# Evictions issued ahead of the background step of a half, and one more step in the gated delta output

## What is computed

```python
def reference(x, ...):                 # x: (1, 256, 2048)
    # block 1
    proj = rms_norm(x) @ w_in          # latent q, kv, rope key, window q/k/v
    h = x + concat(mla_attention(...), swa_sink_attention(...)) @ w_out
    h = h + square(relu(rms_norm(h) @ w_up)) @ w_down          # 2048 -> 8192 -> 2048
    x = rms_norm(h, final_norm)
    # block 2
    proj = rms_norm(x) @ w_in_2        # qkv, z, gates b and a, glu
    o = chunk_gated_delta_rule(q, k, v, g, beta)               # 8 heads of 128
    o = rms_norm(o) * silu(z)
    c = silu(layer_norm(depthwise_conv31(glu)))
    h = x + concat(o, c) @ w_out_2
    h = h + memory_cross_attention(rms_norm(h), rms_norm(mem)) # q, k, v, o: 2048 x 2048
    h = h + square(relu(rms_norm(h) @ w1)) @ w2
    return rms_norm(h)
```

## Time and profile before

| | us |
|---|---|
| median of 3 runs (2673.2 to 2673.64) | 2673.62 |
| the profiled execution | 2671.96 |
| its span, first to last instruction | 2670.2 |
| PE busy in it | 2611.9 |
| DVE busy | 1627.5 |
| ACT busy | 1353.3 |
| mean granted TensorE clock | 0.994 of full |

### The profile page before, as it was taken

One profiled execution on the slowest core, in us unless ns is written; L12 is line 12 of the kernel. 1 busy time (PEld: TensorE's weight loads), 2 busy tenths in 40 slices (PEclk: granted clock), 3 DMA queues, 4 the chain that ended last, 5 costly groups with the idle time before them and its releaser, 6 DMA issues. The chain is left out here.

```text
span 2670.2 us, 31500 instructions
## 1 busy us (share of the span) xinstructions
PE 2611.9 (98%) x12544; PEld 2168.4 (81%) x12544; DVE 1627.5 (61%) x1992; ACT 1353.3 (51%) x1916; POOL 0.2 (0%) x4
## 2 busy tenths in 40 slices
PE   8999999999999999998899999999999999999998
PEld 7877888888888887887888887888888888888886
DVE  6685555555555556567887856644555555555555
ACT  5554544444444446578867644444544444444443
POOL 0000000000000000000000000000000000000000
PEclk9999999999999999999999999999999999999999
DMA  6533665556655654654443327544465566556553
GB/s 219 159 135 134 219 191 192 188 188 190 192 188 187 190 194 151 199 167 157 129 165 113 133 95 267 175 157 143 162 207 189 185 191 194 187 184 192 195 188 134
DMA packets 235241, 468.70 MB, mean 176 GB/s; under 512 B 8187, under 2 KB 17110, under 8 KB 233814
## 3 DMA queue, kind: packets, MB, share of 16 engines
q1 hardware_dynamic: 234806, 466.16, 53.5%
q10 hardware_dynamic: 288, 0.52, 0.1%
HBM read 460.36 MB, written 6.29 MB: 175 GB/s over the span
## 5 line engine op out<-in xcount | busy, mean ns | idle before, releaser
L138 DVE TENSOR_TENSOR WL<-Wt,WH 128x1024 fp32r<-128x1024 f32 (+1 forms) x862 | 1041.7, 1210 | 802.8 <-ACT WH L135 744.1
L135 ACT ACTIVATE WH<-Wt 128x1024 fp32r<-128x1024 f32 (+1 forms) x862 | 898.7, 1046 | 802.7 <-PE ps L168 797.4
L168 PE MATMUL ps<-WH,XT 128*128 128x512 f32 (+1 forms) x3392 | 1087.8, 394 | 4.6 <-DVE WL L138 4.3
L168 PE MATMUL ps<-WH,HT 128*128 128x512 f32 (+2 forms) x3392 | 1059.7, 389 | 2.5 <-DVE WL L138 2.5
L168 PEld LDWEIGHTS ps<-WH,XT 128*128 128x128 f32 x3392 | 638.6, 189 | 136.8 <-DVE WL L138 5.1
L168 PEld LDWEIGHTS ps<-WH,HT 128*128 128x128 f32 x3392 | 636.2, 188 | 128.3 <-DVE WL L138 3.5
L168 PE MATMUL ps<-WL,XT 128*128 128x512 f32 (+1 forms) x1696 | 660.0, 389 | 0.0
L168 PE MATMUL ps<-WL,HT 128*128 128x512 f32 (+2 forms) x1696 | 655.0, 386 | 0.0
L168 PEld LDWEIGHTS ps<-WL,XT 128*128 128x128 f32 x1696 | 320.3, 189 | 62.5 <-issue 1.0
L168 PEld LDWEIGHTS ps<-WL,HT 128*128 128x128 f32 x1696 | 319.7, 189 | 61.5 <-issue 1.0
L138 DVE TENSOR_TENSOR H<-H,ps 128x512 f32<-128x512 f32 x144 | 92.5, 683 | 26.7 <-PE ps L168 26.7
(11 more groups left out here) (262 smaller groups left out, 1301.8 us busy)
## 6 DMA issues: line engine op xcount, KB each, us to landing
Wt<-in_mlp_w SPq DMA_DIRECT2D x128, 1024.0 KB, 5.3
Wt<-in_w_up SPq DMA_DIRECT2D x64, 1024.0 KB, 5.4
Wt<-in_w_down SPq DMA_DIRECT2D x64, 1024.0 KB, 5.0
Wt<-in_w_in SPq DMA_DIRECT2D x53, 1024.0 KB, 5.1
Wt<-in_w_out SPq DMA_DIRECT2D x32, 1024.0 KB, 5.1
Wt<-in_xa_wk SPq DMA_DIRECT2D x16, 1024.0 KB, 5.1
Wt<-in_xa_wv SPq DMA_DIRECT2D x16, 1024.0 KB, 5.0
Wt<-in_xa_wq SPq DMA_DIRECT2D x16, 1024.0 KB, 5.0
```

Source lines behind the costliest of these rows:

```text
L135: return self.p.act.do(lambda e: e.activation(out, in_, func, **kw), w, self.name + "_a")
L138: return self.p.dve.do(lambda e: e.tensor_tensor(out, a, b, op), w, self.name + "_v")
L168: return self.p.pe.do(lambda e: e.matmul(out, l, r, start=start, stop=stop), w, self.name + "_t" if sig else None)
```

## The change

The call of `evac` moves from behind the loop over halves into it, ahead of `pump()`, in the last half of a chunk's last segment. `gen_o` gets one more `yield` between the gate multiply and its transposes.

```diff
@@ gemm
                 pe_free[i] = tok
+                if last_seg and k2 == kb - 2:
+                    gfree[gs] = evac(ci, c0, w, [G[gs][tb][:, 0:w] for tb in range(2)], tok)
                 pump()
-            if last_seg:
-                gfree[gs] = evac(ci, c0, w, [G[gs][tb][:, 0:w] for tb in range(2)], tok)
         return tok
@@ gen_o
         if b == 0:
             return
+        yield
         st = Stage(p, "turn_o")
```

## The result

| | us |
|---|---|
| before, median of 5 runs (2672.04 to 2673.64) | 2673.2 |
| after, median of 5 runs (2805.5 to 2807.98) | 2806.1 |
| ratio, 95% interval | 1.0501 (1.0489 to 1.0513) |
| the profiled execution of after, its span | 2807.63, 2805.8 |

The change makes the kernel 5.0% slower, 133 us; the forecast was 2806. The two profiled executions differ by 2807.63 - 2671.96 = 135.7 us.

A forecast was written before the change was run, and what follows sets the result against it. PE bounds the kernel, busy 2611.9 of 2670.2 us. Terms sum to 109.6 us, 132.0 with the clock; 2671.96 + 132.0 = 2804.0, forecast as a 2806 us median (runs' median 1.7 above the profiled execution), range 2770 to 2845.

The forecast's parts named there:

- The mechanism: Evictions issued ahead of the background step lose the half that covered them, so PE waits in order at the transposes.
- Up chunks: MLP up chunks: transposes of `Vm` wait for the second square, 2.36 us each, 32 chunks, 75.5 us.
- The other chunks: Stalls at `w_out` and `xo` 13.0 us, `w_out_2` 7.0, queries 4.4, last down product of the first MLP 9.3.
- the third rival: Faster: early evictions let transposes and XS work start earlier in the middle of the kernel; at most 2645 us, chance 0.03.
- The clock: After stalls PE's clock can fall, about 1.6 us each; 14 falls of 36 gaps, 22.4 us, bounds 0 and 57.6.
- every gap falls: Rival: every PE gap of 2.2 us or more is followed by a clock fall; 2842 us, chance 0.12.
- the clock holds: Rival: the same stalls on PE but no clock fall; 2784 us, chance 0.12.
- The input product of block 2: `QB` transposes lose 2.76 us of cover, eviction gains 2.28; net 0.48 for 5 chunks, 2.4 us, bounds -10 to +14.
- the eviction is relieved of the background step that stood ahead of it: At `QB`, the early eviction no longer queues on DVE behind `AC` and `QE`, saving 2.28 us.
- The delta output: `VT` transposes: one more half of cover, less `KVS` put ahead; wait from 4.49 to 2.47 us, -2.0 us.
- the DVE queue would stay as it was but for `KVS` put ahead: At the `VT` transposes, early eviction `KVS` adds 0.74 us while the added half takes 2.76 off the wait.
- The short products: Short q and kv products, grouped with all other evictions: same work in another order, 0 us, bounds -5 to +6.

The follow-up runs named there:

- part 2 alone: Against the kernel before: only the added `yield`, one more step ahead of the transposes of `VT`, evictions not moved; 2668.03 us (ratio 0.9984).

## Why the prediction was right, and where it was not

**The mechanism** was right and is shown: the stalls come with the lost half and go with one step, while the order of the evictions stays (2806.1, 2668.4).

**Up chunks**, 2.36 us each, 75.5 in all: the MLP without falls gives 2.34, and 50.1 + 50.2 - 16 x 1.57 = 75.2 in all. The sum of the three parts read from one place of the timeline (slot, end of the eviction, 0.15 us from DVE to PE) held for all 32: the idle times lie between 2.15 and 2.19 us, 2.20 forecast.

**The other chunks**: `w_out` 6.3 us for four (6.5 forecast); `xo` 8.4 - 1.57 = 6.8 (6.5; one of its four stalls is longer, an idle time of 2.46 us, and the fall follows that one); `w_out_2` 5.9 (7.0, here the `XKB` transposes that stand ahead of two of the four fill part of the stall, which I left out); queries 4.9 (4.4, an eviction that ends 0.94 us behind the slot, although the third rival says that the rows show 1.3 to 2.2); last down product of the first MLP 13.1 - 2 x 1.57 = 10.0, of which 0.9 are a wait for `H` that came behind the first matmul of the next product before, so 9.1 (9.3).

**The clock**: 19 more falls, as long as 20, at 1.57 us: 31.4 us, against 14 at 1.6, 22.4. The price was right and the count was not; it was a choice, and the rows on which it rested did not carry it. The limit between 1.91 and 2.13 us that the prediction drew is not there. In the MLPs one half of the stalls fell (16), where I took two in five; three of the four longer ones did, and one in `xo`. The trace of before had more to say than the rows that I chose: behind its first 100 us PE has eight idle times of more than 2 us (2.13, 2.26, 2.38, 2.79, 2.99, 3.22, 3.57 and 4.49 us), and a fall comes with seven of them, all but the one of 3.22. Taken as a rate that speaks for the rival in which every gap falls, so that the choice of two in five came near the half that was measured is luck. The granted clock came out at 0.982, forecast 0.985. The case "every gap falls" did not occur, nor did "the clock holds". The rule that gave the former, of the Trainium skill, page "TensorE: Matmul & The Clock Gate", Part 4, that transposes do not count as busy PE as matmuls do, is not what this kernel shows: 18 transposes in each stall kept the clock at 1.00.

**The input product of block 2**: +7.5 us where 2.4 were forecast. Three falls' worth of it, 4.7 us, is the clock: the fall behind the last down product's fourth stall, and three of its own, as long as four, where before has two. The term itself was for `QB`, and there the waits came out at 9.4 us instead of 10.3, 0.9 less where 2.4 more were forecast. The step that failed is "the eviction is relieved of the background step that stood ahead of it". The generators too start one half earlier, so the long steps `AC` and `QE` keep their place ahead of `QB`. The DVE queue of after, ahead of one `QB`:

```profile
1304.22 1.22 DVE L138 TENSOR_TENSOR AC<-AC,PRD 128x1024 f32<-128x1024 f32 x1
1305.36 1.22 DVE L149 SCALAR_TENSOR_TENSOR QE<-QA,QE 128x1024 f32<-128x1024 f32 x1
1306.49 1.22 DVE L138 TENSOR_TENSOR WL<-Wt,WH 128x1024 fp32r<-128x1024 f32 x1
1307.63 0.74 DVE L145 TENSOR_SCALAR QB<-ps,SM 128x512 f32<-128x512 f32 x1
```

The earlier trace rows have `QB` right behind `AC` and `QE`; now a split stands between. I show this for one of the five. What the stage lost beside the clock lies at other tiles. PE's waits in this stage alone, before:

```profile
PE ps L168 <- DVE WL L138: 2.5, 2, 2.1
PE ps L172 <- DVE QA L138: 1.6, 1, 1.6
```

After:

```profile
PE ps L168 <- DVE WL L138: 4.1, 3, 2.1
PE ps L172 <- DVE GA L138: 2.5, 2, 1.3
PE ps L172 <- DVE QA L138: 2.4, 1, 2.4
```

`GA` is new with 2.5 us; I did not list it although `gate` moves like the others. `WL` has 1.6 more and `QA` 0.8. With `QB` at -0.9 that is 4.0; 0.9 of waits for `H` went to the stage ahead, and 4.0 - 0.9 + 4.7 = 7.8 leaves nothing to look for beside the 7.5. How the falls lie changes from kernel to kernel: the stage varies between 305.4 and 314.0 us over before and the kernels here, with 2 to 4 falls.

**The delta output**: 2.5 us of wait forecast, 1.0 measured; the stage gave back 7.3 us instead of 2.0. The additional step alone does what was said of it, 4.49 to 1.7 us. The step that failed is that the DVE queue would stay as it was but for `KVS` put ahead. `KVS` does stand ahead; but more has moved. Before:

```profile
1610.81 1.22 DVE L138 TENSOR_TENSOR VT<-VT,SM 128x1024 f32<-128x1024 f32 x1
...
1613.08 2.35 DVE L138 TENSOR_TENSOR HT<-LNA,HT 128x1024 fp32r<-128x1024 f32 x2
```

After:

```profile
1680.79 2.35 DVE L138 TENSOR_TENSOR HT<-LNA,HT 128x1024 fp32r<-128x1024 f32 x2
...
1683.06 1.22 DVE L138 TENSOR_TENSOR VT<-VT,SM 128x1024 f32<-128x1024 f32 x1
1685.33 0.75 DVE L145 TENSOR_SCALAR KVS<-ps,SM 128x512 f32<-128x512 f32 x1
1685.99 1.41 DVE L138 TENSOR_TENSOR VT<-VT,ZZ 128x512 f32<-128x512 f32 x2
1687.55 0.63 PE L172 MATMUL ps<-CST,VT 128*128 128x128 f32 x4 [0.99 <-DVE VT L138]
```

The pair `HT<-LNA,HT`, 2.35 us, stood between the two multiplies of `VT` (the earlier trace rows has the second) and now stands ahead of both. The wait of 1.91 us of the earlier trace rows and a fall are gone from the stage too: 3.5 + 1.9 + 1.6 = 7.0 of the 7.3 us. With part 2 alone the wait of 1.9 us is still there, so it went with the early evictions.

**The short products**: forecast 0 with bounds of -5 and +6, measured -2.9: a fall less, the wait of 2.3 us for `CT` gone, and 0.9 for `PC` new.

That the forecast met the median by 0.1 us is therefore partly luck. With the falls (as long as 20, at 1.57, 31.4 us) kept apart from the stages, and the 0.9 us of waits for `H` put back into the input product, the errors against the sum are: falls +9.0; input product 7.5 - 4.7 + 0.9 - 2.4 = +1.3; delta output and memory values -7.3 + 1.6 + 2.0 = -3.7; short products -2.9 + 1.6 = -1.3; `w_out_2` -1.1; the rest, each 0.6 at most, -0.4 together. They add up to +3.8, and 132.0 + 3.8 is, to within 0.1, the measured difference of the profiled executions, 135.7. The terms read from rows of the same place were right to within 1.1 us each. The two that were reasoned through a DVE queue were off by 3.3 (`QB`) and 3.7 us, and the count of falls by 9.0; they met in the sum with opposite signs and with the waits at `GA`, `WL` and `QA`, which no term held.

## What to carry to other kernels

In a kernel whose work is issued as steps between the pieces of one bound engine's stream, the distance in issue order between a result and its first reader is what hides latency. Moving the producers earlier in the list cost nothing here by itself (2673.9 us, before 2672.6), but where a producer also registers its consumer, the consumer moves too, and past the very matmuls that covered it. Ask of every moved call what it appends and where that now runs, and price the lost cover as the end of the producer minus the reader's slot. Where TensorE then stood for some 2 us, about every second stall of this kernel cost another 1.6 us for its clock; that count is to be bounded from all idle times of the trace at hand, not from two of them.

## What the hardware showed that was not expected

A stall of PE can cost more than its length: 32 stalls of 2.34 us cost 75 us, and the 16 falls behind them another 25. Of stalls of equal length half were followed by a fall; what picks them, no run here shows. Idle times of 1.97 and 2.15 to 2.19 us gave the same count, 1.29 us none. Useless work in the stall, four matmuls or 18 transposes, made the kernel 23 to 25 us faster than leaving PE idle there.
